# A mixture-of-experts trunk on one core: gate and up of the last expert moved ahead of six down halves, and the final products given four pairs of banks

## What is computed

```python
def moe_ffn(h, w_router, router_bias, wg, wu, wd):
    t = h.reshape(b * s, d)
    scores = jax.nn.sigmoid((t @ w_router).astype(jnp.float32))
    ...
    combine = jnp.sum(jax.nn.one_hot(idx, N_EXPERTS, dtype=jnp.float32) * gate[..., None], axis=1)
    hg = jnp.einsum('nd,edf->nef', t, wg)
    hu = jnp.einsum('nd,edf->nef', t, wu)
    act = jax.nn.silu(hg) * hu * combine[:, :, None].astype(t.dtype)
    out = jnp.einsum('nef,efd->nd', act, wd)
```

## Time and profile before

| | us |
|---|---|
| median of 3 runs | 1999.18 |
| lowest and highest | 1997.66 and 2003.93 |
| the profiled execution, its own time | 1997.22 |
| its span, first to last instruction | 1995.2 |

### The profile page before, as it was taken

One profiled execution on the slowest core, in us unless ns is written; L12 is line 12 of the kernel. 1 busy time (PEld: TensorE's weight loads), 2 busy tenths in 40 slices (PEclk: granted clock), 3 DMA queues, 4 the chain that ended last, 5 costly groups with the idle time before them and its releaser, 6 DMA issues.

```text
span 1995.2 us, 30643 instructions
## 1 busy us (share of the span) xinstructions
PE 1875.1 (94%) x9018; PEld 1512.8 (76%) x9018; DVE 1588.7 (80%) x2242; ACT 1433.5 (72%) x2279; POOL 85.4 (4%) x86
## 2 busy tenths in 40 slices
PE   7999999997999999999899999999889999999997
PEld 6887888886777777777678878888777777777775
DVE  5556777658999898989874667775689999989897
ACT  5464666446899888889665557664569988889894
POOL 0000000001000000000000000000010000001000
PEclk9999999997999999999999999999889999999999
DMA  7554444556999999999846444445579999999995
GB/s 275 204 189 151 151 151 169 190 211 244 397 404 405 414 399 409 388 396 422 336 178 232 148 166 155 165 148 209 213 278 387 416 408 417 406 402 394 401 411 228
DMA packets 82861, 582.08 MB, mean 292 GB/s; under 512 B 11663, under 2 KB 11919, under 8 KB 13167
## 3 DMA queue, kind: packets, MB, share of 16 engines
q1 hardware_dynamic: 75600, 542.01, 69.8%
q0 software_dynamic: 7168, 38.94, 5.6%
HBM read 575.91 MB, written 29.36 MB: 303 GB/s over the span
## 4 chain that ended last, share of the span: by engine, by line
PE 60%; DMA 16%; issue 8%; ACT 7%; DVE 7%; ACTq 0%; DVEq 0%; SPq 0%
PE bank L851 11%; PE bank L853 11%; PE bank L852 11%; DMA proj<-in_expert_units 9%; DMA raw<-in_expert_units 7%; PE bank L1007 4%; PE bank L1009 4%; PE bank L1023 3%; PE bank L1025 3%; PE bank L1024 3%; ACT wh L573 3%; DVE wl L1202 2%; PE bank L998 2%; DVE xl L1202 1%; ACT rows L784 1%
## 5 line engine op out<-in xcount | busy, mean ns | idle before, releaser
L1194 DVE TENSOR_TENSOR wl<-raw,wh 128x1024 fp32r<-128x1024 f32 x256 | 310.3, 1223 | 226.0 <-ACT wh L564 225.8
L564 ACT ACTIVATE wh<-raw 128x1024 fp32r<-128x1024 f32 x256 | 269.1, 1056 | 262.9 <-PE bank L853 260.7
L851 PE MATMUL bank<-wh,xh 128*128 128x512 f32 x1024 | 415.2, 406 | 2.6 <-DVE wl L1194 2.5
L853 PE MATMUL bank<-wh,xl 128*128 128x512 f32 x1024 | 401.9, 393 | 0.0
L852 PE MATMUL bank<-wl,xh 128*128 128x512 f32 x1024 | 400.3, 391 | 0.0
L1202 DVE TENSOR_TENSOR wl<-raw,wh 128x1024 fp32r<-128x1024 f32 x256 | 302.8, 1220 | 32.9 <-ACT wh L573 31.8
L1202 DVE TENSOR_TENSOR wl<-proj,wh 128x1024 fp32r<-128x1024 f32 x256 | 303.1, 1220 | 28.3 <-ACT wh L573 27.1
L573 ACT ACTIVATE wh<-raw 128x1024 fp32r<-128x1024 f32 x256 | 261.5, 1052 | 54.7 <-PE bank L1025 22.2
L573 ACT ACTIVATE wh<-proj 128x1024 fp32r<-128x1024 f32 x256 | 261.6, 1051 | 47.4 <-PE bank L1025 20.9
L1007 PE MATMUL bank<-wh,xh 128*128 128x512 f32 x648 | 271.6, 419 | 4.5 <-DVE xh L1643 3.0
L1009 PE MATMUL bank<-wl,xh 128*128 128x512 f32 x648 | 263.1, 406 | 0.0
(11 more groups left out here) (245 smaller groups left out, 2712.0 us busy)
## 6 DMA issues: line engine op xcount, KB each, us to landing
raw<-in_expert_units SPq DMA_DIRECT2D x192, 1024.0 KB
proj<-in_expert_units SPq DMA_DIRECT2D x192, 1024.0 KB
raw<-in_in_units SPq DMA_DIRECT2D x96, 1024.0 KB
raw<-in_out_units SPq DMA_DIRECT2D x32, 1024.0 KB
expert_rows<-rows POOLq DMA_DIRECT2D x4, 1024.0 KB, 4.5
proj<-picks POOLq DMA_DIRECT2D x4, 1024.0 KB, 7.9
x<-in_x SPq DMA_DIRECT2D x2, 1024.0 KB, 6.8
wide<-in_norms POOLq DMA_DIRECT2D x2, 1024.0 KB, 5.0
```

The costliest lines, as they stand in the source:

```text
L564: act_(wh[:, h % CUT, :], ring[j][:, h % 2 * HALF:(h % 2 + 1) * HALF], ACT.Copy)\
L851: mm(out, xh[:, at, tok], rh, start=start, stop=False)
L853: return mm(out, xl[:, at, tok], rh, start=False, stop=stop)
L1194: v.tensor_tensor(wl[:, h % CUT, :], ring[(first + h // 2) % slots][:, h % 2 * HALF:(h % 2 + 1) * HALF], wh[:, h % CUT, :].bitcast(F32), A ...
```

## The change

The order of the last step becomes its own, `"last"`: all of gate, two down halves, all of up, six down halves; the eight down halves of the sixteenth expert follow as `"end"`. Gate's and up's ways to act come at new places in that step, ACT waits for the last gate and up half (`half_done`) before it copies, and the high and low parts of the sixteenth expert go into a place of their own in `xh` (`last_actT`). Its down halves use banks 0, 1, 6 and 7 instead of 2 to 5 (`END_BANK`); the four products go to banks 4 and 5, 2 and 3, 0 and 1, 6 and 7. The third group of the next layer's transposes, which uses bank 6, waits for all four column blocks. The host lays out the weights in the new order.

```diff
-PLAN = {True: "g" * PART + "u" * PART, False: "gggguuggddggdduudduudduu", None: "d" * PART}
+PLAN = {"first": "g" * PART + "u" * PART, "mid": "gggguuggddggdduudduudduu",
+        "last": "g" * PART + "dd" + "u" * PART + "dddddd", "end": "d" * PART}
...
+GATE_OUT = {"first": GATED_AT["first"] + DEEP_CUT, "mid": GATED_AT["mid"] + DEEP_CUT, "last": GATED_AT["last"] + 4}
+GATE_SIGMOID = {"first": GATE_OUT["first"] + 1, "mid": GATE_OUT["mid"] + 2, "last": GATE_OUT["last"] + 2}
+GATE_TURN = {"first": GATED_AT["first"] + 2, "mid": GATED_AT["mid"] + 2, "last": GATE_OUT["last"] - 1}
...
+UP_DONE = PLAN["last"].rindex("u")
+LAST_UP_OUT = UP_DONE + 2
+LAST_UP_TURN = UP_DONE + 1
+LAST_GATED = UP_DONE + 3
+LAST_ACT = UP_DONE + 5
-JOIN_BANK = (0, 6, 0, 2)
+END_BANK = (0, 1, 6, 7)
+JOIN_BANK = (4, 2, 0, 6)
...
+                def half_done(n, h):
+
+                    e.wait_ge(S["cut_free"], t_.ahead("cut_free", n + DEEP_CUT - h))
+
...
+                            if kind == "last":
+                                half_done(GATED_AT[kind], h)
                             gate_out()
...
+                        if h == LAST_UP_OUT and kind == "last":
+                            half_done(UP_DONE, h)
+                            up_out()
+                        if h == LAST_ACT and kind == "last":
+                            act_hi((SLOTS,), last_actT)
...
                     for h in range(PART):
-                        part_cut(h, 4)
-                        if h in (UP_OUT - 2, UP_OUT - 1):
-                            store(0, h - UP_OUT + 2, NE - 2)
-                        if h == UP_OUT:
-                            up_out()
-                            for k in (2, 3):
-                                store(0, k, NE - 2)
-                            act_hi((SLOTS,))
-                    e.wait_ge(S["cut_free"], t_.ahead("cut_free", DEEP_CUT))
+                        part_cut(h, 4, "end")
+                    for k in range(4):
+                        store(0, k, NE - 2)
+                    for k in range(4):
+                        if k % 2 == 0:
+                            half_done(PART - 2 + k // 2, PART - 1)
+                        last_store(k)
                     t_.due("cut_free", DEEP_CUT - CUT)
-                    for k in range(4):
-                        last_store(k)
...
+                    if g == 2:
+
+                        e.wait_ge(S["x_cols"], t_.ahead("x_cols", 2))
...
                     t_.decide()
                     for h in range(PART):
-                        part_cut(h, 4)
-                        if h == UP_OUT:
-                            gated()
-                            act_lo((0, STACK), SLOTS)
-                            add_picks(0)
+                        part_cut(h, 4, "end")
+                    add_picks(0)
```

More of the change, by code:

```diff
@@ L131 @@
 MIX_BANK = (0, 1, 0, 1, 2, 3, 2, 3)
-XT = {False: {PART + 3: 0, 2 * PART: 1}, True: {2: 0, PART: 1}}
+XT = {"mid": {PART + 3: 0, 2 * PART: 1}, "first": {2: 0, PART: 1}, "last": {}}
 XT_MOVE = {f: {h + DEEP_CUT + 1: g for h, g in at.items()} for f, at in XT.items()}
@@ L565, in cut, with part_cut @@
                     .then_inc(S["hi_ready"], 1)
-            def part_cut(h, at, first=False):
+            def part_cut(h, at, kind):
                 j = (at + h // 2) % DEEP
@@ L572, in part_cut @@
                 e.wait_ge(S["cut_free"], t_.due("cut_free"))
-                act_(high[part_slot(h, first)], ring[j][:, h % 2 * HALF:(h % 2 + 1) * HALF], ACT.Copy)\
+                act_(high[part_slot(h, kind)], ring[j][:, h % 2 * HALF:(h % 2 + 1) * HALF], ACT.Copy)\
                     .then_inc(S["hi_ready"], 1)
@@ L792, in last_store, with step @@
                         e.wait_ge(S["out_free"], t_.due("out_free"))
-                    act_(last_rows[:, k * COLS:(k + 1) * COLS], bank[2 + k][SLOTS:STACK, :], ACT.Copy,
+                    act_(last_rows[:, k * COLS:(k + 1) * COLS], bank[END_BANK[k]][SLOTS:STACK, :], ACT.Copy,
                          scale=last_weight[SLOTS:STACK, 2:3]).then_inc(S["last_out"], 1)
[L796 to L800, removed]
+                def step(b, k, kind, stores=True):
+                    at = 0 if kind == "first" or b == 1 else 4
+                    for h in range(len(PLAN[kind])):
+                        part_cut(h, at, kind)
+                        if h == DEEP_CUT - 1 and kind == "first":
@@ L1019, in down_half @@
                 k = h // 2
+                left_of = last_actT if end else actT
                 for c in range(2):
                     r = slice(c * COLS, (c + 1) * COLS)
-                    o = bank[2 + 2 * (h % 2) + c][:, :]
-                    mm(o, actT[:, k, 0:STACK], high[j][:, r], start=(k == 0), stop=False)
-                    mm(o, actT[:, k, 0:STACK], low[j][:, r], start=False, stop=False)
-                    last = mm(o, actT[:, k, SLOTS:SLOTS + STACK], high[j][:, r], start=False, stop=(k == 3))
+                    n = 2 * (h % 2) + c
+                    o = bank[END_BANK[n] if end else 2 + n][:, :]
+                    mm(o, left_of[:, k, 0:STACK], high[j][:, r], start=(k == 0), stop=False)
+                    mm(o, left_of[:, k, 0:STACK], low[j][:, r], start=False, stop=False)
+                    last = mm(o, left_of[:, k, SLOTS:SLOTS + STACK], high[j][:, r], start=False, stop=(k == 3))
                 last.then_inc(S["cut_free"], 1)
@@ L1732, in ask_again, with step @@
                     e.wait_ge(S["dve_done"], t_.due("dve_done"))
-                def step(b, first=False, last=False):
-                    at = 0 if first or b == 1 else 4
-                    for h in range(len(PLAN[first])):
-                        part_cut(h, at, first)
-                        if h == DEEP_CUT - 1 and first:
+                def step(b, kind):
+                    at = 0 if kind == "first" or b == 1 else 4
+                    for h in range(len(PLAN[kind])):
+                        part_cut(h, at, kind)
+                        if h == DEEP_CUT - 1 and kind == "first":
                             for g in range(2):
                                 rows_lo(0, g, (7, 5)[g])
-                        if h == TABLES and first:
+                        if h == TABLES and kind == "first":
                             tables(FIRST, NE)
@@ L1811 @@
         taken = {"g": iter(range(F // P)), "u": iter(range(F // P)), "d": iter(range(F // P))}
-        for part in PLAN[False][::2]:
+        for part in PLAN["mid" if k < NE - 1 else "last"][::2]:
             n = next(taken[part])
```

116 lines of the change are left out of this document (60 added, 56 removed).

## The result

The changed kernel takes **1986.3 us** (median of 5 runs, 1984.46 to 1990.67) against 1999.18: 0.9941 of the kernel before, 95% interval 0.9924 to 0.9959. Measured again in another set it was 1986.83, ratio 0.9949 (0.9933 to 0.9964). The profiled execution took 1984.46, its span is 1982.7.

What follows compares the result with a forecast made beforehand. PE's gap and low clock at each layer's end were taken to bound the kernel, DVE's picks and pairs next. Gains of 6.9 and 6.6 us, less 1.7 and 0.2, gave -11.6: 1987.5 us, range 1982 to 1994.

Steps and rivals of the forecast that it cites:

- PE: Layer ends: the gap before the sixteenth expert's downs goes; second layer's downs end at 1974.8 instead of 1981.97, first layer's 9.1 us earlier.
- The two waits added on ACT: ACT waits for the eighth gate half and eighth up half before copying: costs 0.3 us on PE, 1.0 on DVE.
- The lead did not run out: Rival: ACT's waits cost DVE the whole 3 us, each layer gains 2 to 3 less; about 1992.5 us, chance 0.15.
- DVE, and thus the end, first layer: First layer's end: third and fourth picks land at 988.55, four pairs end at 998.2 instead of 1005.04; gain 6.9 us.
- DVE, second layer: Second layer's end: third and fourth picks end at 1979.65, four pairs at 1984.65 instead of 1991.27; gain 6.6 us.
- one of the signs named for a wrong prediction: At the layer ends: the prediction is wrong if the picks land later than now; no size given.
- The output: From the last pair to the span's end, 3.9 us before: closer pairs add 0.2 us, between 0 and 0.5.
- The layer boundary: Between the layers: PE idles and the low clock behind it costs 1.7 us, between 0 and 3.4.
- The sum: Whole kernel: -6.9 - 6.6 + 1.7 + 0.2 = -11.6 us; 1987.5 us against the median.
- Slower: Rival: clock stays low after the layer boundary, the dense projection loses 15.5 us; about 2001 us, chance 0.04.
- Nothing is gained: Rival: weight units land later by what PE saves, so the end stays; 1998 to 2000 us, chance 0.08.
- the change doesn't do what it says: Rival: act late, PE waits at first end half; about 1.5 us (second layer) and 4 (first) free; no chance given.

Runs made afterwards that it cites:

- all the old banks: The changed kernel's new order of halves with the banks, store places and store waits of the kernel before: 1998.33 us, 0.9992 of the kernel before.
- the late picks: Adding of the third and fourth block of picks left out: on the changed kernel 1980.01 us (0.9907), on the kernel before 1999.83 us (1.0009).

## Why the prediction was right, point by point

The forecast of 1987.5 us lies 1.2 above the median, and its likeliest case is the one that came. By its own steps:

- *PE.* The down halves were to end 9.1 and 7.2 us earlier; counted from the folding they did by 9.3 and 7.2. The chain through act costs nothing, at full clock. With four downs as cover PE still does not wait.
- *The two waits added on ACT.* The lead did not run out: no PE wait of the kind taken at 0.3. The 1.0 us on DVE is not to be seen apart.
- *DVE, and thus the end, first layer:* 6.9 forecast, 7.2 measured. Landing near 988.6 was forecast, and the third pick started on landing at 987.00, that is 988.2 on the clock of before (its folding is 1.23 us earlier here). But "the landing binds" is only half right: DVE's own floor is 1.1 us below that, and some executions run at it.
- *DVE, second layer:* 6.6 forecast, 5.4 measured. The step that was mis-sized is the landing. I left POOL's issue at its time before, and the stream's phase against PE's moved: the last read was issued 31.60 us behind the folding instead of 29.69, so the third pick waited until 40.3 behind it, where I had 39.0. Of this 1.3 us, 0.4 is DVE's own work (39.4 where nothing waits), 0.9 the landing. By the folding these picks landed 1.4 us later than before (40.3 against 38.9), so one of the signs named for a wrong prediction came by half; by the span's own time they landed 7 us earlier. POOL's row of after:

```profile
1959.06 0.54 POOL L552 DMA_DIRECT2D wide<-picks  x1
```

- *The output:* 0.2 forecast, 1.4 measured. The sum took 390 GB/s from a window of loads; the stores in rows of 2 KB move 294. With pairs every 1.72 us that had nearly sufficed; at 1.22 each block adds to the queue.
- *The layer boundary:* 1.7 forecast between 0 and 3.4; 0.5 and 2.3 measured in two profiles of one kernel, 1.4 in the mean of the nine profiles with a low clock there. The size was right in the mean. The reason given, that 1.33 us of idling brings no slow matmuls, does not carry far: with all the old banks the clock fell behind the same wait of 1.33 us, with one of 1.12 some 7 us ahead of it.
- *The sum:* -11.6 forecast. By the parts shown it is -10.7 in the first profile, and the two timings give -11.8 and -10.2 (1 less the ratio, times 1999). Two terms erred against the change (2.4 us together). That the forecast still came out 1.2 from the median is in part luck: in the first profile the boundary was 1.2 cheaper than forecast, and 1.8 us came from steps that both kernels share.
- *The rivals.* "Slower" needed a low clock of some 27 us; it was 3 to 7. "Nothing is gained" fell with the first pair. Under "the change doesn't do what it says" I wrote that a PE wait at the first end half would be mostly free, 1.5 us in the second layer and 4 in the first. **That step was wrong**, and luck that it was not called on: the end downs in the old banks make just that wait, 3.6 us, and the first pair came 3.5 and 3.7 later. Two things were left out. The clock falls behind the wait, so PE's products are 6.4 and 6.7 us late and not 3.6, past the 4.4 and 2.9 us of slack that they have. And there is no such slack towards the weight slots: these feed ACT's cuts, the cuts DVE's subtractions, and the picks stand behind the subtractions. At the first pair the second is the dearer by 1.4 to 1.7 us; at the last pair the two can't be told apart.
- *The banks.* I gave them no price of their own. By the runs, without them the new order is worth nothing (0.9992).

## What to carry to other kernels

Slack belongs to a path, not to an engine: before calling a stall free, follow each thing that the stalled engine releases, its slots and banks too, to whoever sits behind it in another engine's queue. And take it at each consumer: here it was 4.4 us at the first pair and 2.9 at the last. When a change moves the bound from one engine to the next, take the new bound's work away in both kernels, as with the late picks: free in one and dear in the other shows the handover. And count positions from a landmark close by, since whole executions differ by more than such parts are worth.

## What was not expected of the hardware

Stores of the same 2.10 MB took 7.1 us of all DMA engines in 1152 packets and 5.3 in 576. The low clock behind one and the same idle wait at the boundary lasted 3 to 4 us in one execution and about 7 in another, worth 1.8 us in the end. What brings it is not settled: behind a wait of 1.33 us it stayed at 1.00 in the kernel before; with all the old banks it fell behind such a wait, where one of 1.12 had gone some 7 us ahead.
